# A two-block fp32 transformer on one core: the router on the raw state, and the order of layer 1's first products, splits and scalings

## What is computed

```python
def rms_norm(x, g):
    y = xf * lax.rsqrt(jnp.mean(xf * xf, -1, keepdims=True) + EPS)
    return (y * g.astype(jnp.float32)).astype(x.dtype)
...
        h = h + g1 * y                       # first_block, each layer
        h = h + g2 * ffn(rms_norm(h, norm2_g[l]) * (1 + sc2) + sh2)
...
def moe_swiglu(x, router, w1, w3, w2):       # the ffn of layer 1
    logits = (xt @ router).astype(jnp.float32)
    top_v, top_i = lax.top_k(logits, TOP_K)  # 2 of 8
    top_w = jax.nn.softmax(top_v, axis=-1)
    gates = jnp.sum(jax.nn.one_hot(top_i, N_EXPERTS) * top_w[..., None], axis=1)
    for e in range(N_EXPERTS):
        out = out + gates[:, e:e + 1] * swiglu(xt, w1[e], w3[e], w2[e])
```

## Time and profile before

| | |
|---|---|
| runs, median (lowest to highest) | 1799.89 us (1798.51 to 1800.46) |
| profiled execution: its own time | 1800.71 us |
| its span in the trace | 1798.5 us |
| mean granted TensorE clock | 0.962 |
| PE busy | 1669.8 us, 93% |
| DVE busy | 1239.5 us, 69% |
| ACT busy | 832.8 us, 46% |
| POOL busy | 144.8 us, 8% |

### The profile page before, as it was taken

One profiled execution on the slowest core, in us unless ns is written; L12 is line 12 of the kernel. 1 busy time (PEld: TensorE's weight loads), 2 busy tenths in 40 slices (PEclk: granted clock), 3 DMA queues, 4 the chain that ended last, 5 costly groups with the idle time before them and its releaser, 6 DMA issues. The chain is left out here.

```text
span 1798.5 us, 21440 instructions
## 1 busy us (share of the span) xinstructions
PE 1669.8 (93%) x8686; PEld 1423.7 (79%) x8686; DVE 1239.5 (69%) x1618; ACT 832.8 (46%) x1015; POOL 144.8 (8%) x152
## 2 busy tenths in 40 slices
PE   5999988999999998798799999999989788989998
PEld 3778877888888887797688788887779667779986
DVE  6578854587565536767689898889976465566643
ACT  6354433322122325334467677667654334545532
POOL 2110102000110022310100000000300000000000
PEclk9999989999999998998799999999999899889999
DMA  8344423355565422211479898988865422135553
GB/s 338 96 164 133 155 90 116 141 197 195 205 257 187 173 68 94 71 48 48 164 256 345 298 359 326 335 325 321 324 216 179 141 82 94 65 135 187 188 187 117
DMA packets 60504, 333.60 MB, mean 185 GB/s; under 512 B 14690, under 2 KB 15009, under 8 KB 28400
## 3 DMA queue, kind: packets, MB, share of 16 engines
q1 hardware_dynamic: 54640, 311.06, 47.6%
q0 software_dynamic: 4032, 14.57, 2.6%
q10 hardware_dynamic: 1728, 6.54, 1.0%
HBM read 331.00 MB, written 1.13 MB: 185 GB/s over the span
## 5 line engine op out<-in xcount | busy, mean ns | idle before, releaser
L2133 DVE TENSOR_TENSOR wlo__61<-raw__60,whi__62 128x2048 fp32r<-128x2048 f32 (+2 forms) x64 | 145.2, 2269 | 72.7 <-ACT whi__62 L1566 72.5
L2133 DVE TENSOR_TENSOR wlo__65<-raw__64,whi__66 128x2048 fp32r<-128x2048 f32 (+3 forms) x64 | 141.1, 2204 | 73.2 <-ACT whi__66 L1566 73.2
L1566 ACT ACTIVATE whi__62<-raw__60 128x2048 fp32r<-128x2048 f32 (+2 forms) x64 | 118.9, 1858 | 88.9 <-DMA raw__60<-in_ffn_w 42.4
L1566 ACT ACTIVATE whi__66<-raw__64 128x2048 fp32r<-128x2048 f32 (+3 forms) x64 | 115.3, 1802 | 82.2 <-DMA raw__64<-in_ffn_w 29.5
L2133 DVE TENSOR_TENSOR wlo__69<-raw__68,whi__70 128x2048 fp32r<-128x2048 f32 (+4 forms) x50 | 109.2, 2185 | 31.0 <-ACT whi__70 L1566 30.9
L2169 DVE SCALAR_TENSOR_TENSOR wsum__71<-raw__68,silu_rows 128x1024 f32<-128x1024 f32 x84 | 99.9, 1219 | 1.4 <-DMA raw__68<-in_ada_w 0.9
L3297 POOL TENSOR_TENSOR keep__58<-keep__58,keep__59 128x1 f32<-128x1 f32 (+3 forms) x48 | 51.6, 1079 | 593.4 <-DVE keep__58 L2210 593.3
L1566 ACT ACTIVATE whi__70<-raw__68 128x2048 fp32r<-128x2048 f32 (+4 forms) x50 | 90.4, 1808 | 15.8 <-DMA raw__68<-in_w_ff 11.6
L2133 DVE TENSOR_TENSOR wlo__235<-raw__234,whi__236 128x2048 fp32r<-128x2048 f32 (+1 forms) x24 | 50.6, 2110 | 11.8 <-ACT whi__236 L1566 11.8
L2427 DVE TENSOR_REDUCE keep__58<-ps 128x1 f32<-128x256 f32 (+1 forms) x88 | 44.5, 517 | 18.5 <-PE ps L1182 9.9
L2133 DVE TENSOR_TENSOR wlo__231<-raw__230,whi__232 128x2048 fp32r<-128x2048 f32 (+1 forms) x24 | 52.7, 2197 | 0.0
(11 more groups left out here) (1169 smaller groups left out, 5326.9 us busy)
## 6 DMA issues: line engine op xcount, KB each, us to landing
raw__68<-in_moe_w SPq DMA_DIRECT2D x24, 1024.0 KB, 5.0
raw__60<-in_moe_w SPq DMA_DIRECT2D x24, 1024.0 KB, 5.4
raw__68<-in_ada_w SPq DMA_DIRECT2D x16, 1024.0 KB, 4.9
raw__64<-in_moe_w SPq DMA_DIRECT2D x16, 1024.0 KB, 5.2
raw__230<-in_moe_w SPq DMA_DIRECT2D x16, 1024.0 KB, 5.9
raw__234<-in_moe_w SPq DMA_DIRECT2D x16, 1024.0 KB, 6.4
raw__144<-in_ada_w SPq DMA_DIRECT2D x13, 1024.0 KB, 6.2
raw__68<-in_ada_w POOLq DMA_DIRECT2D x20, 512.0 KB, 4.1
```

The costliest lines, as they stand in the source:

```text
L1566: e.activation(t.hi(), t.raw(), ACT.Copy).then_inc(*did("hi", i))
L2133: e.tensor_tensor(t.lo(), t.raw(), t.hi().bitcast(F32), ALU.subtract).then_inc(*did("lo", i))
```

## The change

- **Norm "f":** the split of the third weight tile stands ahead of the square and scaling of the last token tile.
- **Start of layer 1:** the first 16 steps of the fill stand ahead of the turns of `cq`; DVE splits `wlo65` right behind the means; both cosine products come ahead of both sums, and POOL makes both row factors first. `ck` is written doubled by one instruction, without the 16 copies; the four copies of `cv` move from DVE to ACT. One `dk` bank moves to another PSUM ring.
- **Router:** the raw state is turned, behind the last output product, without waiting for the row factor. Gain alone is applied. Since (r·h·gain + shift)·R = r·((h·gain)·R) + shift·R, the row factor r is applied to the logits, and a shift row is added. That row comes from 8 new products of the shift (which POOL copies into `XSm[1]` at full width) with the router's weights. The row scaling of the state, still needed for the gather, goes from DVE to ACT. The two splits and two low halves leave the stretch ahead of the logits: `wlo69` goes ahead of the last two gatings, the low halves behind the choice and behind the first one-hots, `wlo61` behind those. The eight small gate operations stand behind the first expert's third hidden step, and the one-hots of the experts 2 to 7 inside it.
- **Experts 6 and 7:** the product of `MACC` with the row and the addition are eight POOL instructions of 512 columns, spread over expert 6; expert 6 is scaled at its output too (two more DVE instructions of 128x512).
- **a3:** the two splits stand several steps apart.
- **Block 2, start:** the first product uses another PSUM ring.

The core of the diff:

```diff
-                        b = take("c", "od", kind, hf, p)
+                        b = take("t" if (kind, hf, p) == ("dk", 0, 0) else "c", "od", kind, hf, p)
...
+        fill = paired()
+        advance(fill, 16)
         for t in range(2):
             head_turn(("cq", t), XR[t], 4, [("orot", "cq", t)], "h")
-        fill = paired()
-        advance(fill, HEADS["a1"].begun)
+        advance(fill, HEADS["a1"].begun - 16)
         for t in range(4):
             head_turn(("ck", t), XR[(2 + t) % 4][:, 128:384], 2, [("orot", "ck", t)], "x")
...
+        def state_turned(t, half):
+            for s, n in due(h_done(("o", 1), t)[half]):
+                e.wait_ge(s, n)
+            for k in range(half * 4, half * 4 + 4):
                 o = k % 2 * 256 + t * 128
-                m = tr(bank("mt", k - k % 2)[:, o:o + 128], XSm[t][:, k * 128:(k + 1) * 128])
+                m = tr(bank("mt", k - k % 2)[:, o:o + 128], h_t[t][:, k * 128:(k + 1) * 128])
                 if k % 2 and t:
                     m.then_inc(*done("mt", k - 1))
-        bs = [take("6", "router", t) for t in range(2)]
+        state_turned(0, 0)
...
+        state_turned(0, 1)
+        b = take("h", "shift")
+        for s, n in due(("shb",), ("rw",)):
+            e.wait_ge(s, n)
+        for k in range(KT):
+            m = e.matmul(b[:, 0:8], XSm[1][:, k * 128:(k + 1) * 128], RW[:, k, :], start=k == 0, stop=k == KT - 1)
+        m.then_inc(*done("shift"))
+        state_turned(1, 1)
         for k in range(KT):
             for t in range(2):
-                for s, n in due(("mx_a" if k & 2 else "mx_v", k - k % 2), ("rw",)):
+                for s, n in due(("mx_a" if k & 2 else "mx_v", k - k % 2)):
                     e.wait_ge(s, n)
                 m = e.matmul(bs[t][:, 0:8], XT32[:, k, t * 128:(t + 1) * 128], RW[:, k, :], start=k == 0,
                              stop=k == KT - 1)
                 if k == KT - 1:
                     m.then_inc(*done("router", t))
...
+        feed(("prod", "o", 1, 0, 0))
         at["ahead"] = 2
-        for t in range(2):
-            for s, n in due(*h_done(("o", 1), t)):
+        feed(("prod", "o", 1, 0, 1))
...
             for k in (k0, k0 + 1):
-                m = e.activation(XT32[:, k, :], bank("mt", k0)[:, (k - k0) * 256:(k - k0) * 256 + 256], ACT.Identity,
-                                 scale=sc2b[:, 2 * k:2 * k + 1], bias=sh2b[:, 2 * k:2 * k + 1])
+                m = e.activation(XT32[:, k, :], bank("mt", k0)[:, (k - k0) * 256:(k - k0) * 256 + 256], ACT.Copy,
+                                 scale=sc2b[:, 2 * k:2 * k + 1])
...
+
+        def state_scaled(t):
+            for s, n in due(("mrs", t)):
+                e.wait_ge(s, n)
+            e.activation(XSm[t], h_t[t], ACT.Copy, scale=SS[:, t:t + 1]).then_inc(*did("mxn", t))
             high("mxh", (t,), XSP[t][0], XSm[t], ("mxn", t))
-        at["slots"].update(slot_m)
-        at.update(ahead=3, idle=True)
-        feed(("mt", 6))
+        state_square(0)
+        state_gained(2)
+        state_square(1, ("shift",))
+        state_gained(6)
+        for s, n in due(("shift",)):
+            e.wait_ge(s, n)
+        e.activation(R0, bank("shift")[:, 0:8], ACT.Copy).then_inc(*did("r0"))
+        empties(("shift",), ("r0",))
+        state_scaled(0)
         for s, n in due(("mdf",)):
             e.wait_ge(s, n)
         e.activation(two8(MD)[:, :, 3], two8(MD)[:, :, 2], ACT.Exp).then_inc(*did("mexp"))
-        at["ahead"] = 4
+        state_scaled(1)
+        at["slots"].update(slot_m)
+        at.update(ahead=3, idle=True)
         feed(("rank",))
         at.update(ahead=2, idle=False)
...
-                     *([("yg", r, ex, half)] if r or ex == 7 else [("y", r, ex, 10)]), *xg_free(r, ex, "scat", 1, 1))
+                     *([("yg", r, ex, half)] if r or ex > 5 else [("y", r, ex, 10)]), *xg_free(r, ex, "scat", 1, 1))
...
+            if st == "a3":
+                at["ahead"] = 0
             for i in A.steps():
-                if st == "a3":
-                    at["ahead"] = 2 if i > A.lag + 2 else 0
...
+                if st == "a3" and i - A.lag in (4, 9):
+                    at["ahead"] = 1 + (i - A.lag) // 9
+                    feed(("score", st, i, 0))
+                    at["ahead"] -= i - A.lag == 4
...
         at["ahead"] = 2
+        feed(("nt", "f", 0, 6))
         norm_scale("f", 3)
...
+        at["ahead"] = 2
+        feed(("prod", "od", "cq", 1))
         for t in range(2):
             odd_scale("cq", t)
-            odd_rotate("cq", t)
-        at["ahead"] = 2
...
-            e.tensor_scalar(XSm[t], h_t[t], SS[:, t:t + 1], None, ALU.mult).then_inc(*did("mxn", t))
-        for k0 in (0, 4):
...
             for s, n in due(("mt", k0), ("gain", "n2b", 0), ("prod", "o", 1, 1, 1)):
                 e.wait_ge(s, n)
             for k in (k0, k0 + 1):
                 m = e.tensor_scalar(XT32[:, k, :], bank("mt", k0)[:, (k - k0) * 256:(k - k0) * 256 + 256],
-                                    sc2b[:, 2 * k:2 * k + 1], sh2b[:, 2 * k:2 * k + 1], ALU.mult, ALU.add)
+                                    sc2b[:, 2 * k:2 * k + 1], None, ALU.mult)
...
-            m = e.tensor_copy(LG[:, t * 8:t * 8 + 8], bank("router", t)[:, 0:8])
+            means("mms", (t,), SS[:, t:t + 1], D, ("msq", t))
+        for t in range(2):
+            for s, n in due(("router", t), ("mrs", t), ("r0",)):
+                e.wait_ge(s, n)
+            m = e.scalar_tensor_tensor(out=LG[:, t * 8:t * 8 + 8], in0=bank("router", t)[:, 0:8], scalar=SS[:, t:t + 1],
+                                       in1=R0, op0=ALU.mult, op1=ALU.add)
             m.then_inc(*link())
             empties(("router", t), ("v", at["chain"]))
...
             w_, g = (128, 1) if key[0] == "ckv" else (512, dict(cq=0, dq=2, dk=3)[key[0]])
-            rsqrt("hrs", key, SSN[c % 8][:, 0:w_ // 64], ("hms", *key))
+            for c_, unit in [(0, ODD_UNITS[0]), (1, ODD_UNITS[1])] if c == 0 else [(c, key)] if c > 1 else []:
+                rsqrt("hrs", unit, SSN[c_ % 8][:, 0:w_ // 64], ("hms", *unit))
...
+            e.wait_ge(s, n)
+        e.tensor_copy(v3(XSm[1], KT), sh2b.rearrange("p (k v) -> p k v", v=2)[:, :, 0:1].broadcast_to([128, KT, 128])).then_inc(
+            *did("shb"))
         for half in range(2):
...
-            e.tensor_tensor(MACC[t], MACC[t], GBC[:, D:2 * D], ALU.mult).then_inc(*did("hgate", t))
-            for s, n in due(("hgate", t)):
-                e.wait_ge(s, n)
-            e.tensor_tensor(h_t[t], h_t[t], MACC[t], ALU.add).then_inc(*did("hpre", t))
+        for t in range(2):
+            rsqrt("mrs", (t,), SS[:, t:t + 1], ("mms", t))
+        for t in range(2):
+            for half in range(2):
+                hs, gs = (slice(o + half * 512, o + half * 512 + 512) for o in (0, D))
+                pace = [("acc", 0, 5, 1, 1), ("hid", 0, 6, 2, 4, "3"), ("y", 0, 6, 2), ("y", 0, 6, 6)][2 * t + half]
+                for s, n in due(("acc", 0, 5, t, half), pace, *spr(11)):
+                    e.wait_ge(s, n)
+                e.tensor_tensor(MACC[t][:, hs], MACC[t][:, hs], GBC[:, gs], ALU.mult).then_inc(*did("hgate", t, half))
```

More of the change, by code:

```diff
@@ L153 @@
     "post_v": ("pms", "post", "pyo", "r2"),
-    "turn": ("gt", "nt", "ht", "mt", "mqt"), "route": ("router", "rank"), "slot_in": ("gp", "gx", "scat"),
+    "turn": ("gt", "nt", "ht", "mt", "mqt"), "route": ("router", "rank", "shift"), "slot_in": ("gp", "gx", "scat"),
     "mods": ("mod", "spread"),
@@ L1336, in tensor_program @@
                     m.then_inc(*done("router", t))
-        b = take("6", "rank")
+        turn_of["6"] += 3
+        b = take("h", "rank")
         for s, n in due(("sel",)):
@@ L1823, in odd_square, with odd_value @@
             e.activation(SQ[c % 2][:, 0:w_], bank("od", *key)[:, 0:w_], ACT.Square).then_inc(*did("hsq", *key))
+        def odd_value(t):
+            for s, n in due(("hn", "ckv", t)):
+                e.wait_ge(s, n)
+            e.activation(CV[:, t, :], bank("od", "ckv", t)[:, 128:256], ACT.Copy).then_inc(*did("cv2", t))
+            empties(("od", "ckv", t), ("cv2", t))
         def odd_hi(kind, t, dst, n_):
@@ L2800, in vector_program @@
                 odd_rotate("ckv", t - 1)
-        for t in range(4):
-            odd_value(t)
         at["ahead"] = 0
@@ L2910, in onehots @@
                 e.tensor_scalar(SHR, RANK, float(CAP), None, ALU.subtract).then_inc(*link())
-            for ex in range(2) if first else range(2, 8):
+            for ex in exs:
                 for t in range(2):
@@ L3008, in output_lo @@
         def output_lo(r, ex):
-            for half in range(2) if r or ex == 7 else ():
+            for half in range(2) if r or ex > 5 else ():
                 for s, n in due(("y", r, ex, 10), *spr(11)):
```

179 lines of the change are left out of this document (98 added, 81 removed).

## The result

The change ran in 1758.06 us (median of 4 runs, 1755.4 to 1762.83) against 1799.7 before (the mean of the middle two of its four runs; the 1799.89 above is the upper one): ratio 0.9772, 95% interval 0.9747 to 0.9797. It is 41.6 us faster; 26 were forecast, and 1766 was the lower end of the range. The direction was right, the size was not.

The account below looks back on a forecast made before the run. PE was taken as the bound, busy 1669.8 of 1798.5 us, losing time to idle waits and half clock. Terms of 4 + 5.5 + 7 + 2 + 7.5 = 26 us off 1800.7 gave about 1775, range 1770 to 1781.

Parts of the forecast that it names:

- At nothing: Edits priced at zero: block 2's first bank, the cosines beyond what is counted, the one-hots moved into expert 0.
- block 2's first bank: Start of block 2: moving the first product to another PSUM ring was priced at nothing.
- rival 2: All five priced places at their upper bounds, 34.3 us, so 1766; chance 0.09.
- the five known places: Norm "f", start of layer 1, router, experts 6 and 7, a3: 4 + 5.5 + 7 + 2 + 7.5 = 26 us.
- norm "f": At 314.47: PE's 2.42 us wait for split wlo69 and the half clock behind it go; 4 us (2.4 to 4.1).
- start of layer 1: From 704: PE's stalls before the cq turns and wlo65 go, DVE's chain limits the gain; 5.5 us (2 to 8.4).
- router, to the gather: Output projection's end to first gather product, today 22.95 us: 6.6 earlier by its sum, taken as 7 (2.3 to 9.5).
- experts 6 and 7: 1283 to 1304: spreading POOL's work over expert 6 eases the stall of DVE stretched by POOL; 2 us (-2 to 3.8).
- a3: PE's 3.06 us wait behind two splits shrinks by 2.0, half clock from 1540.00 to 1553.50 goes; 7.5 us (1 to 8.5).
- Nearly all at 0.50: Claim that the 22.95 us from the output projection's end to the first gather product ran nearly all at half clock.
- Rival 1: At all five places: waits go but low clock stays, granted a little later; 13.5 us, so 1787; chance 0.19.
- Rival 4: First expert: splits left behind the gather make PE pause repeatedly, clock stays low; slower, 1805 at 60 us; chance 0.04 with the like.

Follow-up runs that it names:

- The test on DVE: Whole change with the old order of experts 6 and 7, MACC's product and addition moved from POOL to DVE in eight instructions: 1753.55 us, ratio to before 0.9751.

## Why the prediction was wrong, point by point

**The step that failed** is the paragraph *At nothing*, and in it "block 2's first bank". I had priced a change of PSUM bank as a change of name. It moves the phase of a ring of eight for all that follows, and took 9.66 and 4.28 us of PE's waiting away, 17.5 with the clock. The two rows stood in the trace of before, 9.66 as the largest wait of PE behind its first 16 us, 4.28 as the fourth. The forecast went through the waits "at the places that the diff touches" and took these as places that it does not touch. The question to ask of a wait is not whether its instruction is in the diff, but which of the things it waits for (operands, weights, the bank it writes) the diff moves. Here the operands were there; what DVE released was the bank. No rival held it either, and rival 2, the end of the range, only took the five known places at their upper bounds. Nor was it a matter of the five being too small: without the ring part they gave 24.7 us, for the 26 of the forecast.

The other steps, forecast against the whole change in its place, and the part alone:

| step | forecast | in the change | alone |
|---|---|---|---|
| norm "f" | 4 | 5.0 | 4.4 |
| start of layer 1 | 5.5 | 4.5 | 4.8 |
| router, to the gather | 7 | 8.5 | 7.3 |
| experts 6 and 7 (by taking them out) | 2 | 0 | not run |
| block 2's first bank | 0 | 17.5 | 17.5 |
| a3 | 7.5 | 6.8 | 6.9 |

- **Norm, layer 1, a3:** right in size, and in mechanism as far as the waits go; the clock's share at the norm may be luck. In layer 1 the give-back came at DVE's `ck`, as expected. The 4.50 of the earlier trace rows became the 1.96 for `wlo61`, 2.5 less where the forecast had 1.2, and the 0.94 for an exponential grew to 3.61, which it did not have.
- **Router:** right; 7 forecast (6.6 by its sum), 6.0 to 8.5 in six traces. The logits took 3.83 us in the change, near the full-clock end (3.5), but 4.96 to 6.18 in the other five. The choice and the low half cost what they did before. 1.3 were given back in the first expert. "Nearly all at 0.50" was too much for the 22.95 us: the 0.50 begins at 881.20, 4.2 us into them. No term hangs on it.
- **Experts 6 and 7:** the term was mis-sized, 2 for 0. The Trainium skill ("SBUF — State Buffer", "Who interferes with whom") has the port pair of DVE and GpSimd as an exclusive lock held for the whole instruction, and the forecast had drawn 0 or slightly below from it. The traces agree with the blocking and with the 0, but not with a lock that is as long in eight pieces as in four: DVE lost 4.9 us for 7.7. What the term had for itself, slack in expert 6, was there for the first halves; the last ones stretched the splits in front of the new scaling, and the 3.8 us of PE's waits that went came back as 4.2. The test on DVE shows it from the other side: without POOL the stretch has 3.6 us more.
- **Rival 1** (the clock stays low) came in part: the low clock went at the norm and at a3, but at the start of layer 1 and at the router it stayed, shorter than before (the longest stretches are 6.8 and 13.7 us; before they were 10.2 and 23.9, worked out from the earlier trace rows). Windows of the changed kernel:

```profile
716.00:722.80 6.80, 4.24 (x16) 3.57 (x17) 5.49 (x11) 0.98 (x3) 4.50 (x3) 0.50 0.01 2
873.00:886.70 13.70, 9.79 (x45) 9.23 (x45) 11.67 (x28) 8.97 (x11) 0.00 (x0) 0.50 0.41 167
```

- **Rival 4** did not come: the first expert ran at a clock of 0.99 from 885 to 960.

## What to carry to other kernels

A change of buffer, ring or bank index is a change of dependencies for everything that is allocated after it: list, for each large wait of the kernel before, what holds the buffer that the waiting instruction writes, and look whether the change moves it. When parts are timed one by one, compare the start of the same instruction in both timelines, place by place: the medians of single parts here add up to 52 us (7.0 + 8.0 + 11.3 + 9.1 + 16.8) where the whole gave 41.6, since each of the five but the last holds 2 to 4 us that its own place doesn't show. And a helper engine that stretches the engine it helps can cost more than it spares: 3.6 us in its place here, in one pair of traces, though not in the times of the whole kernels.
